# Hybrid decoder trunk on one core: the scan's side work in another order, and the masked C·B product in SBUF

## The reference

```python
seg = a_cs[..., :, None] - a_cs[..., None, :]
decay = jnp.exp(jnp.where(causal, seg, -jnp.inf))
cb = jnp.einsum('bclgn,bcsgn->bcgls', Cc, Bc)
y_diag = jnp.einsum('bcgls,bcghls,bcsghp->bclghp', cb, decay, xdt)
states = jnp.einsum('bclgn,bcghl,bclghp->bcghpn', Bc, decay_states, xdt)
# h_next = h * chunk_decay + states, chunk after chunk
y_off = jnp.einsum('bclgn,bcghpn,bcghl->bclghp', Cc, prev, jnp.exp(a_cs))
y = y.reshape(b, s, SSD_INNER) * jax.nn.silu(z)        # then a grouped RMSNorm
return y.astype(u.dtype) @ w_out                       # output projection
```

## Time and profile before

| | us |
|---|---|
| median of 3 runs (2294.07 to 2297.25) | 2294.2 |
| profiled execution, its own time | 2294.51 |
| span of the profiled execution | 2292.8 |
| PE busy in the span | 2252.1 (98%) |
| POOL, DVE, ACT busy | 1369.2, 1297.7, 1114.8 |

### The profile page before, as it was taken

One profiled execution on the slowest core, in us unless ns is written; L12 is line 12 of the kernel. 1 busy time (PEld: TensorE's weight loads), 2 busy tenths in 40 slices (PEclk: granted clock), 3 DMA queues, 4 the chain that ended last, 5 costly groups with the idle time before them and its releaser, 6 DMA issues.

```text
span 2292.8 us, 29155 instructions
## 1 busy us (share of the span) xinstructions
PE 2252.1 (98%) x10626; PEld 1838.5 (80%) x10626; DVE 1297.7 (57%) x1730; ACT 1114.8 (49%) x2044; POOL 1369.2 (60%) x1020
## 2 busy tenths in 40 slices
PE   8999999999999999999999989999999999999998
PEld 6877888888888878888888767778888888888887
DVE  7356663333336897831355668878763333336787
ACT  4046543333333446654455686766543333333445
POOL 3224288777773664787776244342388777774554
PEclk9999999999999999999999999999999999999999
DMA  5110322323228755143332455342322323228744
GB/s 163 46 28 19 120 77 99 120 88 119 88 101 285 256 157 170 74 130 116 110 117 84 165 191 177 121 156 93 120 85 90 120 88 120 88 103 291 250 148 159
DMA packets 169466, 294.06 MB, mean 128 GB/s; under 512 B 19424, under 2 KB 98156, under 8 KB 166764
## 3 DMA queue, kind: packets, MB, share of 16 engines
q1 hardware_dynamic: 165740, 280.26, 36.1%
q10 hardware_dynamic: 3584, 11.93, 1.3%
HBM read 216.00 MB, written 76.15 MB: 127 GB/s over the span
## 4 chain that ended last, share of the span: by engine, by line
PE 86%; DVE 6%; ACT 3%; DMA 2%; issue 2%; POOL 1%; SPq 0%; DVEq 0%; ACTq 0%; POOLq 0%
PE ps L2377 49%; PE ps L2090 5%; PE ps L2092 5%; PE ps L2091 5%; PE ps L2467 5%; PE ps L2471 5%; PE ps L2463 5%; DMA w_raw<-in_ssd_w_out 1%; PE ps L2113 1%; PE ps L2535 1%; PE ps L2818 1%; ACT mdec L2030 1%; DVE d_lo L3118 1%; PE ps L2808 1%; PE ps L2300 1%
## 5 line engine op out<-in xcount | busy, mean ns | idle before, releaser
L1157 POOL TENSOR_TENSOR s_lo<-s_val,s_hi 128x512 fp32r<-128x512 f32 x154 | 234.6, 1529 | 199.0 <-ACT s_hi L1697 198.4
L3066 DVE TENSOR_TENSOR xres<-ps,xres 128x512 f32<-128x512 f32 x132 | 90.6, 688 | 401.1 <-PE ps L2377 401.1
L1078 POOL TENSOR_TENSOR p_lo<-p_val,p_hi 128x512 fp32r<-128x512 f32 x176 | 239.4, 1369 | 48.8 <-ACT p_hi L1502 37.8
L1502 ACT ACTIVATE p_hi<-p_val 128x512 fp32r<-128x512 f32 x176 | 111.0, 632 | 308.3 <-POOL p_val L1104 308.3
L2377 PE MATMUL ps<-xn_hi,p_hi 128*128 128x512 f32 x704 | 188.9, 390 | 1.3 <-ACT xres L1605 1.3
L2377 PE MATMUL ps<-xn_lo,p_hi 128*128 128x512 f32 x704 | 188.2, 389 | 0.0
L2377 PE MATMUL ps<-xn_hi,p_lo 128*128 128x512 f32 x704 | 188.2, 389 | 0.0
L1697 ACT ACTIVATE s_hi<-s_val 128x512 fp32r<-128x512 f32 x154 | 96.9, 629 | 150.2 <-DMA d_val<-in_w_down 87.7
L2377 PEld LDWEIGHTS ps<-xn_hi,p_hi 128*128 128x128 f32 x704 | 131.6, 188 | 28.9 <-ACT p_hi L1502 2.0
L2377 PEld LDWEIGHTS ps<-xn_hi,p_lo 128*128 128x128 f32 x704 | 132.2, 188 | 27.5
L2377 PEld LDWEIGHTS ps<-xn_lo,p_hi 128*128 128x128 f32 x704 | 132.2, 188 | 27.5
(11 more groups left out here) (414 smaller groups left out, 5697.6 us busy)
## 6 DMA issues: line engine op xcount, KB each, us to landing
s_val<-hidden SPq DMA_DIRECT2D x154, 256.0 KB, 2.9
hidden<-xres SPq DMA_DIRECT2D x20, 1792.0 KB, 6.4
wv_g<-in_w_gate SPq DMA_DIRECT2D x22, 1024.0 KB, 5.1
wv_u<-in_w_up SPq DMA_DIRECT2D x20, 1024.0 KB, 5.1
d_val<-in_w_down SPq DMA_DIRECT2D x70, 256.0 KB, 4.0
rows_v<-in_w_down SPq DMA_DIRECT2D x64, 256.0 KB, 3.7
mdec<-decay_sums SPq DMA_DIRECT2D x32, 512.0 KB, 4.2
xres<-parked_x SPq DMA_DIRECT2D x24, 512.0 KB, 6.7
```

Source lines behind the costliest of these rows:

```text
L1078: pool.tensor_tensor(p_lo[n][:, :, :], src, f(p_hi[n][:, :, :]), ALU.subtract).then_inc(p_lo_done, 1)
L1157: pool.tensor_tensor(s_lo[i][:, :], s_val[i][:, :], f(s_hi[i][:, :]), ALU.subtract)\
L1502: act.activation(p_hi[n][:, :, :], src, ACT.Copy).then_inc(p_hi_done, 1)
```

## The change

The masked product moves from PSUM to two small SBUF buffers `cbm`, used in turn, and `masked_decay` reads it there. Bank CB is then free once DVE has masked and copied it, so PE's wait for `m_ready` in `token_major` is dropped; `masked_decay` keeps its own wait. The number of instructions of this part is the same.

The order of the side work is rewritten on four queues. `gated` and `split` of half a sequence are cut in two parts of two blocks each, placed in two chunks; roots, high parts and low parts of weight pieces stand behind other chunks; SP issues the pieces 4 and 5 of group 0 earlier, and two residual tiles (`load_back(6, 7)`) later. `Q_BLOCKS` ends with a block of z in place of one of x, so the two rows that are finished in the scan (`is_late`) need no taps on DVE: ACT copies them out of PSUM, and takes the Silu later.

```diff
+        cbm = [at(f"cbm{i}", 4736 + i * P, [P]) for i in range(2)]
...
-        SILU_AFTER_CHUNK = {1: (0, 1), 3: (2, 3), 5: (4, 5), 7: (6,)}
+        SILU_AFTER_CHUNK = {1: (0, 1), 3: (2, 3), 5: (4, 5)}
...
-        PIECE_HI = [{0: 2, 1: 3, 3: 4, 4: 5, 5: 6, 6: 7}, {1: 0, 3: 1, 4: 2, 6: 3}, {0: 0, 2: 1, 4: 2, 6: 3}, {0: 0, 2: 1}]
...
+        PIECE_HI = [{0: 2, 1: 3, 2: 4, 4: 5, 6: 6, 7: 7}, {1: 0, 3: 1, 6: 2, 7: 3}, {2: 0, 3: 1, 6: 2, 7: 3}, {2: 0, 3: 1}]
+        SPLITS = [{6: (0, 0, (0, 1)), 7: (0, 0, (2, 3))},
+                  {2: (0, 1, (0, 1)), 3: (0, 1, (2, 3)), 5: (1, 0, (0, 1)), 6: (1, 0, (2, 3))}]
+        SPLITS += [{1: (g_ - 1, 1, (0, 1)), 2: (g_ - 1, 1, (2, 3)), 5: (g_, 0, (0, 1)), 6: (g_, 0, (2, 3))}
+                   for g_ in range(2, G)]
+
+        LO_AHEAD = [{1: ((2, 0),), 2: ((3, 0),), 3: ((4, 0),), 5: ((5, 0),), 7: ((6, 0), (6, 1))},
+                    {2: ((0, 0),), 4: ((1, 0),), 7: ((2, 0), (2, 1))},
+                    {3: ((0, 0),), 4: ((1, 0),), 7: ((2, 0), (2, 1))},
+                    {3: ((0, 0),), 4: ((1, 0),)}]
+        LO_BEHIND = [{1: ((2, 1),), 2: ((3, 1),), 3: ((4, 1),), 5: ((5, 1),), 7: ((7, 0), (7, 1))},
+                     {2: ((0, 1),), 4: ((1, 1),), 7: ((3, 0), (3, 1))},
+                     {3: ((0, 1),), 4: ((1, 1),), 7: ((3, 0), (3, 1))},
+                     {3: ((0, 1),), 4: ((1, 1),)}]
...
-        Q_BLOCKS = ([(0, "x0"), (0, "x1")] + [(g, n) for g in range(1, G) for n in ("z0", "z1")]
-                    + [(g, n) for g in range(1, G) for n in ("bc", "x0", "x1")])
+        Q_BLOCKS = ([(0, "x0"), (0, "x1")] + [(g, n) for g in range(1, G) for n in ("z0", "z1")][:-1]
+                    + [(g, n) for g in range(1, G) for n in ("bc", "x0", "x1")] + [(G - 1, "z1")])
...
                     load_decay(c + 2)
+                    if c == 0:
+                        load_piece(0, 4)
                     if c == 1:
+                        load_piece(0, 5)
                         sp.wait_ge(gc_ready, 1)
                         load_back(0, 1)
-                    if c == 2:
-                        load_piece(0, 4)
                     if c == 3:
-                        store_row(row_at(NQ - 1, "g", 1))
-                        store_row(row_at(NQ - 1, "g", 2))
-                        load_piece(0, 5)
-                    if c == 4:
                         load_piece(0, 6)
                     if c == 5:
                         for i in range(4):
-                            sp.wait_ge(row_stored[i], 16 * ((len(ROWS) - 1 - i) // 4 + 1))
+                            sp.wait_ge(row_stored[i], 16 * ((len(ROWS) - 3 - i) // 4 + 1))
                         load_bc(1, 0)
                         sp.wait_ge(z_full, 5)
                         load_xrows(1, 0)
                         load_piece(0, 7)
-                        load_back(6, 7)
+                    if c == 6:
+                        store_row(row_at(NQ - 1, "g", 1))
+                        store_row(row_at(NQ - 1, "g", 2))
...
                         load_xrows(g, 1)
+                    if c == 1:
                         load_piece(g, 1)
...
                         load_piece(g, 2)
+                        if g == 1:
+                            for i in (2, 3):
+                                sp.wait_ge(row_stored[i], 16 * ((len(ROWS) - 1 - i) // 4 + 1))
+                            load_back(6, 7)
...
+                if is_late(i):
+                    act.activation(row_buffer(i), flat(row_banks(i)), ACT.Copy).then_inc(tap0_done, 1)
+                    return
...
+                    if (g, c) in ((0, 0), (0, 1)):
+                        next_hi(g, PIECE_HI[g][c])
                     if g == 0:
                         for u in SILU_AFTER_CHUNK.get(c, ()):
                             silu_z(u)
-                    if (g, c) == (0, 1):
+                    if (g, c) == (0, 3):
                         row_silu(row_at(NQ - 1, "g", 1))
+                    if (g, c) == (0, 5):
                         row_silu(row_at(NQ - 1, "g", 2))
                     if (g, c) == (1, 0):
+                        silu_z(ZU - 2)
                         silu_z(ZU - 1)
-                        root(0)
-                    if (g, c) == (1, 2) or g >= 2 and c == 1:
-                        split(g - 1, 1)
-                    if (g, c) == (0, 6) or g and c == 5:
-                        split(g, 0)
-                    if c in PIECE_HI[g]:
+                    if g and c == 0:
+                        root(2 * g - 2)
+                    if g and c == 4:
+                        root(2 * g - 1)
+                    if c in SPLITS[g]:
+                        split(*SPLITS[g][c])
+                    if c in PIECE_HI[g] and (g or c > 1):
                         next_hi(g, PIECE_HI[g][c])
-                    if (g, c) == (1, 4):
-                        root(1)
-                    if g >= 2 and c == 3:
-                        root(2 * g - 1)
-                    if g and c == 7:
+                    if g == G - 1 and c == 7:
                         root(2 * g)
...
                     pe.wait_ge(cb_freed, k)
-                    pe.wait_ge(m_ready, 2 * k)
                 ins = pe.matmul(ps[:, CB, 0:P], BT[:, tok], CT[:, tok], start=True, stop=True)
...
-                ins = dve.tensor_tensor(ps[:, CB, 0:P], ps[:, CB, 0:P], f(tri[:, :]), ALU.mult)
+                ins = dve.tensor_tensor(cbm[c % 2][:, :], ps[:, CB, 0:P], f(tri[:, :]), ALU.mult)
...
+                first, second = (0, 1), (2, 3)
                 if g == 0:
-                    if c == 6:
+                    if c == 5:
                         gated(0, 0)
-                    if c == 7:
-                        rests(0, 0, range(BG - 1))
                     return
                 if c == 0:
                     if g == 1:
-                        rest(0, 0, BG - 1)
+                        rests(0, 0)
                     else:
                         add_tile(g - 2, NT - 1)
-                        reciprocal_rms(2 * g - 2)
-                        gated(g - 1, 1)
-                elif (g, c) == (1, 1):
-                    reciprocal_rms(0)
-                elif (g, c) == (1, 5):
-                    reciprocal_rms(1)
-                elif g >= 2 and c == 4:
+                        rest(g - 1, 0, BG - 1)
+                        gated(g - 1, 1, first)
+                    return
+                if c == 1:
+                    reciprocal_rms(2 * g - 2)
+                elif c == 5:
                     reciprocal_rms(2 * g - 1)
-                if c:
-                    add_tile(g - 1, c - 1)
-                if (g, c) == (1, 1):
-                    gated(0, 1)
+                add_tile(g - 1, c - 1)
+                if g == 1:
+                    if c == 1:
+                        gated(0, 1, first)
+                    elif c == 2:
+                        gated(0, 1, second)
+                    elif c == 4:
+                        rests(0, 1)
+                elif c == 1:
+                    gated(g - 1, 1, second)
+                elif c == 3:
+                    rests(g - 1, 1, range(BG - 1))
+                elif c == 4:
+                    rest(g - 1, 1, BG - 1)
                 if c == 4:
-                    if g == 1:
-                        rests(0, 1)
-                    gated(g, 0)
-                if g >= 2 and c == 3:
-                    rests(g - 1, 1)
-                if c == 7:
-                    rests(g, 0)
+                    gated(g, 0, first)
+                elif c == 5:
+                    gated(g, 0, second)
+                elif c == 7:
+                    rests(g, 0, range(BG - 1))
...
-                        dve.tensor_tensor(four, four, ps[:, CB, 0:P].unsqueeze(1).to_broadcast([P, 4, P]), ALU.mult)\
+                        dve.tensor_tensor(four, four, cbm[c % 2][:, :].unsqueeze(1).to_broadcast([P, 4, P]), ALU.mult)\
...
+            rest(G - 1, 0, BG - 1)
             gated(G - 1, 1)
```

More of the change, by code:

```diff
@@ L537, in is_z, with is_late @@
             return ROWS[i][1] >= NCB
+        def is_late(i):
+            return i >= len(ROWS) - 2
         def of_kind(i):
@@ L1313, in ssd_group @@
                     if c in LO_AHEAD[g]:
-                        b, half = LO_AHEAD[g][c]
                         pool.wait_ge(cb_full, NT * g + c + 1)
@@ L1317, in ssd_group @@
                             pool.wait_ge(q_full, q_order.count(0, NQ - 1, "M4g"))
-                        half_lo(piece(b), half)
+                        for b, half in LO_AHEAD[g][c]:
+                            half_lo(piece(b), half)
                     if c < NT - 1:
@@ L1330, in ssd_group @@
                     if c in LO_BEHIND[g]:
-                        b, half = LO_BEHIND[g][c]
-                        half_lo(piece(b), half)
+                        for b, half in LO_BEHIND[g][c]:
+                            half_lo(piece(b), half)
                 t.add("chunk", NT)
@@ L1770, in row_silu @@
             def row_silu(i):
```

(14 more changed lines are left out.)

4 lines of the change are left out of this document (1 added, 3 removed), and 3 rows, old and new, of the table LO_AHEAD.

## The result

The changed kernel takes 2263.95 us (median of 4 runs, 2263.59 to 2265.25), the kernel before 2294.31 beside it. The ratio is 0.9866, 95% interval 0.9849 to 0.9883: 30.4 us faster. The forecast was 2271 in a range from 2267 to 2284.

The account below looks back on a forecast made before the run. PE, the busiest engine, was taken to bound the kernel, losing time in the scan to mask waits and slow clock: −18.7 − 8 + 1.4 + 1.4 + 0.7 = −23.2 us, so 2271 us, range 2267 to 2284.

Parts of the forecast that it names:

- slow clock: PE in the scan runs partly at 1.2 instead of 2.4 GHz behind four stalls; removing this gives about 8 us.
- The ceiling of 26.7 us: All that PE's stalls in the scan can give back: 18.7 us idle plus 8 of slow clock; faster than 2267: chance 0.02.
- The dropped wait: PE at the C·B product no longer waits for masks; alone 12.6 us of stalls and about 4 of slow clock.
- rival 1: Order gives less than the sum, ACT staying late at a chunk 7 or two: 2278, range 2275 to 2284, chance 0.22.
- The order: Moved side work on ACT, DVE and SP in the scan must give the other 6.1 us of the stalls.
- Where a stall is left: group 0: PE's waits around chunks 7 to 9: one stall left, 1.4 us, plus 1.4 allowed for load times.
- Masks in SBUF: DVE's 64 masked decays meet POOL: 0.15 us each, 10 us of DVE time, hidden except 0.7 us on the path.
- Rivals 2 and 4: POOL holds up the masks: at 1.1 us each about 2298, chance 0.05; at 0.9 each 2284 to 2290, chance 0.07.
- rival 3: No real change, PE waiting as long at the diagonal part as before at C·B: 2292 to 2295, chance 0.04.
- Taps in the projections: Taps on two rows leave the scan's start for the projections, where PE has no visible wait: 0 us.

Follow-up runs that it names:

- e8: Kernel before, old order, with the masked product in SBUF, PE's wait kept and POOL's sums of squares cut to 8 of 512 columns: 2295.01 us.
- e11: Kernel before, old order, with the masked product in SBUF, PE's wait dropped and POOL's sums of squares cut to 8 of 512 columns: 2278.53 us.
- e1: Kernel before, old order, with the masked product in SBUF and PE's wait for the masks dropped, POOL's sums full: 2281.29 us.
- e7: Changed kernel with POOL's sums of squares in the scan cut to 8 of 512 columns: 2264.62 us.
- The three parts that I undid: Changed kernel with late weight pieces earlier (2266.26 us), gate products and splits uncut (2267.98), group 0's pieces 4 to 6 at old places (2266.0); all at once 2272.58.
- e4: Kernel before, old order, with the masked product in SBUF and nothing else changed, PE's wait kept: 2299.09 us.

## Why the direction was right, and which step of the size failed

**The sum against the ruler.** The forecast of 23.2 us was 15.2 of stalls (18.7 less 3.5) and 8 of slow clock. The ruler has 18.2 of stalls, 8.3 of slow clock and 2.8 that the sum had no term for, 29.3 in all; the last 1.1 to the 30.4 of the medians lie outside the ruler, and no run ascribes them to the change. So of the 7.2 us that were missing 3.0 are the 3.5 put on stalls that would be left, and 2.8 are the small parts. The ceiling of 26.7 us for all that the stalls can give back, on which the chance of 0.02 below 2267 rested, was too low for the same reason.

**The dropped wait: right in its sum, not in its two parts.** 16.6 us forecast in the old order, 16.5 measured where POOL's sums hold up no mask (e8 to e11; against the kernel before, which lacks e8's stall at product 2 and its slow clock at product 14, e11 gains 15.0); rival 1, built on this term without the order, put 2278, and e11 took 2278.5, though with full sums it is e1's 2281.3. That the sum fits is luck, since its two parts are off in opposite directions. I had 12.6 of stalls and 4 of slow clock, and measured are 8.2 of stalls (20.2 to 12.0) and so 8.3 of slow clock and small parts. I had taken 1.75 or 2.61 us off each stall by itself. Stalls are not independent: PE without the earlier ones comes sooner to chunk 7, whose mask ACT's chain sets, and waits there 6.21 us in e11, more than the 5.07 of e8.

**The order: right in kind, too small.** The forecast gave it 6.1 us of stalls and 4 of slow clock, less 3.5 of allowances. From e11 to e7, with small sums on both sides, it is 13.9 us, and from e1 to the changed kernel 17.3. By the ruler the 13.9 are 14.7: 11.5 of stalls (12.0 to 0.5), where I had 2.6, and 3.2 of slow clock and small parts. So the order removes the 4.4 us of stalls too that I had put on the dropped wait. Most of the 3.4 us between the two figures (2.4 by the ruler) are POOL's sums, which the new order moves off PE's path. The three parts that I undid account for 8.6 us together; the rest (roots, Silus, SP's other loads) was not taken apart.

**The step that failed: "Where a stall is left: group 0".** It put 1.4 us on one stall, 1.4 on load times, and 0.7 on masks that meet POOL at that border, 3.5 in all; the trace shows 0.5. The schedule itself was good. The masks of k = 7 and 8 came 0.55 and 0.06 us before PE wanted them, where I had 0.8 and 0.3, and that of k = 9 came 0.47 late, where the schedule had 0.8. The last one in the changed kernel, on ACT, DVE and PE:

```profile
1352.20 1.28 ACT L1974 ACT_TABLE_LOAD   x1
1353.49 1.09 ACT L1974 ACTIVATE z_first<-ps 128x512 f32<-128x512 f32 x2
1354.60 1.28 ACT L2001 ACT_TABLE_LOAD   x1
...
1361.26 1.15 ACT L2056 ACTIVATE mdec<-mdec 128x512 f32<-128x512 f32 x2
```

```profile
1361.92 1.29 DVE L3656 TENSOR_TENSOR mdec<-mdec,cbm 128x512 f32<-128x512 f32 x2 [3.19 <-ACT mdec L2056]
```

```profile
1363.27 1.09 PE L2841 MATMUL ps<-mdec,xdt 128*64 128x128 f32 x16 [0.47 <-DVE mdec L3656]
```

ACT took 10.2 us from 1352.20 to the end of the Exp (1361.26 + 1.15), just as I had. What I then added, 0.6 for a Silu that might wait for PE, 1.4 for load times and 0.7 for POOL, did not come: here ACT waits neither for a load nor for PE, and the mask pair takes 1.29 us. These were risks, and their place was the range, not the sum. With the 0.3 by which this mask was less late than in the schedule, that is the 3.0 us.

**Terms left out.** The small parts come to 2.8 us. In eight steps with a stall PE took 0.13 to 0.26 us longer than the idle time in them explains (three are in the table above), 1.5 in all. Two steps without a stall, 17 to 18 and 25 to 26, each one step behind a slow one, were 0.31 longer; the rest is 0.1 or less a step. I had taken the idle time for the whole stall and didn't compare steps between equal points. What PE does in that time is not settled. The 1.9 us before the scan are a difference between two executions, not part of the change; in the medians it is hidden in their spread.

**Masks in SBUF: right for this order, for the wrong reason.** The price of 0.15 us each was 0.195 (682 to 877 ns), and it stayed off the path (e7). But my argument was that the tail is rare. It is not rare where it matters: in the old order it cost 4 to 6 us (e4 against e8 and against before), because ACT's weight copy releases POOL's run 4.2 us ahead of the mask pair of chunk 7, the run of low parts and full sums is about 7 us long, and PE waits for that pair. (My expectation for e8 put both releases at the same time; the rows of e1 show the 4.2 us.) With full sums the dropped wait is worth 17.8 us (e4 to e1), of which the operand's place takes back 5.8 (before to e4), so the change of buffer without a change of order brings 12. Rivals 2 and 4 fell, since 0.2 us more for each mask is far from the 0.6 more at which their sum begins to cost, and rival 3, by e1 and the result.

**Taps in the projections: nothing, as forecast.** Kernels with the old projections reach the first C·B at 1283.54 to 1285.29, those with the new at 1283.02 to 1285.64.

## What to carry to other kernels

Two measures against the same stall are not additive: the order alone is worth 25 us, the new buffer with the dropped wait alone 12 to 13, both 30. Stalls on one engine are not independent either: where another engine's chain sets the time, removing the earlier ones can make a later one longer (5.07 to 6.21 us here). Price a stall by the step between two equal instructions, with and without it: idle time was only 18.2 of the 29.3 us. When an operand moves from PSUM to SBUF, look at which instruction of GpSimd runs at the moment when the waited-for VectorE instruction starts, not at how busy GpSimd is in the mean. And a term for what might go wrong belongs in the range unless a row puts it on the path.
